# Attention products turned round: values stationary, probabilities moving, row sums divided out by a diagonal in the transposes

## The reference, cut to what matters

```python
proj = rmsnorm(x, g_mix) @ w_in            # q_a, k_a, v_a, c_q, c_kv, k_pe, gate_a, gate_b
y_a = moba_attention(q_a, k_a, v_a)        # 8 heads of 64; with 256 tokens: one causal block
y_b = causal_attention(q_b, k_b, v_b)      # 8 heads, 96 features in q and k, 64 in v
# each head: probs = softmax(where(causal, q @ k.T * scale, -inf)); y = probs @ v
merged = sigmoid(gate_a) * (y_a @ w_branch_a) + sigmoid(gate_b) * (y_b @ w_branch_b)
x = x + merged @ w_out
x = x + routed_experts(rmsnorm(x, g_ffn), ...)   # top 4 of 32, every expert's 12 MB read
```

## Time and profile before

| | |
|---|---|
| median of 3 runs | 1439.06 us (1436.78 to 1440.57) |
| the profiled execution's own time | 1436.58 us |
| its span in the profile | 1434.2 us |
| PE busy in the span | 1360.7 us (95%) |
| DVE busy | 423.4 us (30%) |
| ACT busy | 274.7 us (19%) |
| mean HBM traffic | 348 GB/s |

### The profile page before, as it was taken

How to read it: one execution, slowest core, us unless ns; L and a number is a source line. 1 busy time by engine, 2 the same in 40 slices (tenths; PEclk the granted TensorE clock), 3 DMA queues, 4 the chain that set the end, 5 groups by cost and what they waited for, 6 DMA issues and landing times.

```text
span 1434.2 us, 16180 instructions
## 1 busy us (share of the span) xinstructions
PE 1360.7 (95%) x6618; PEld 678.6 (47%) x6618; DVE 423.4 (30%) x661; ACT 274.7 (19%) x392; POOL 30.7 (2%) x50
## 2 busy tenths in 40 slices
PE   8999999999999999999999898999999989999898
PEld 4446644433433343343333333333333336898896
DVE  2344323311211121121112111121112116775774
ACT  2133213110110111111101011010111114532531
POOL 2100010000000000000000000000000000000000
PEclk9999999999999999999999999999999999999999
DMA  9992377899999999999999999999999996355330
GB/s 329 387 341 88 118 265 321 361 416 426 429 428 428 429 429 428 429 428 428 429 428 430 428 430 427 429 429 428 430 428 429 428 413 238 126 179 199 122 124 30
DMA packets 76972, 498.71 MB, mean 348 GB/s; under 512 B 7095, under 2 KB 8586, under 8 KB 52362
## 3 DMA queue, kind: packets, MB, share of 16 engines
q1 hardware_dynamic: 75802, 496.06, 84.6%
q0 software_dynamic: 704, 2.10, 0.4%
q10 hardware_dynamic: 432, 0.07, 0.0%
HBM read 497.06 MB, written 1.05 MB: 347 GB/s over the span
## 4 chain that ended last, share of the span: by engine, by line
PE 69%; DMA 24%; DVE 4%; ACT 2%; issue 1%; POOL 0%; SPq 0%; ACTq 0%; DVEq 0%
PE ps L1621 31%; DMA ring<-in_w_gate_up_dram 24%; PE ps L1386 7%; PE ps L1731 5%; PE ps L1733 5%; PE ps L1732 5%; PE ps L1615 3%; PE ps L1552 2%; PE ps L1536 2%; PE ps L1396 2%; PE ps L1602 1%; PE ps L1686 1%; ACT arena L688 1%; PE ps L1625 1%; PE ps L1365 1%
## 5 line engine op out<-in xcount | busy, mean ns | idle before, releaser
L1621 PE MATMUL ps<-ring,arena 128*64 128x512 f32 x2304 | 515.3, 598 | 28.2 <-DMA ring<-in_w_gate_up_dram 17.1
L1621 PEld LDWEIGHTS ps<-ring,arena 128*64 128x64 f32 x2304 | 159.5, 137 | 356.5 <-issue 304.7
L1621 PE MATMUL ps<-arena 128*64 128x512 f32 x768 | 177.9, 616 | 5.0 <-ACT arena L688 3.1
L1130 DVE TENSOR_SCALAR arena<-ps 128x512 f32<-128x512 f32 x32 | 22.1, 692 | 342.5 <-PE ps L1621 342.5
L681 ACT ACTIVATE arena<-arena 128x512 f32<-128x512 f32 x32 | 20.2, 630 | 491.4 <-DVE arena L1130 491.4
L1386 PE MATMUL ps<-ring,HT 128*128 128x512 f32 (+1 forms) x256 | 111.3, 586 | 1.3 <-ACT HT L594 1.0
L1621 PEld LDWEIGHTS ps<-arena 128*64 128x64 f32 x768 | 54.2, 141 | 119.5 <-issue 105.0
L1733 PE MATMUL ps<-arena_highs,w_low 128*128 128x256 f32 x384 | 108.5, 282 | 0.0
L1091 DVE TENSOR_SCALAR esel<-const 128x128 fp32r<-128x128 f32 x49 | 12.6, 285 | 281.4 <-ACT arena L692 143.5
L692 ACT COPY arena<-ps 64x512 f32<-64x512 f32 x64 | 37.1, 580 | 241.0 <-PE ps L1621 240.6
L1109 DVE TENSOR_TENSOR X<-X,ps 128x1024 f32<-128x1024 f32 x34 | 41.4, 1218 | 121.5 <-PE ps L1615 121.5
(11 more groups left out here) (246 smaller groups left out, 1341.2 us busy)
## 6 DMA issues: line engine op xcount, KB each, us to landing
ring<-in_w_gate_up_dram SPq DMA_DIRECT2D x96, 2048.0 KB, 31.0
ring<-in_w_down_dram SPq DMA_DIRECT2D x48, 2048.0 KB, 33.7
arena<-in_w_gate_up_dram SPq DMA_DIRECT2D x32, 2048.0 KB, 30.7
ring<-in_w_in_dram SPq DMA_DIRECT2D x38, 1024.0 KB, 6.9
arena<-in_w_down_dram SPq DMA_DIRECT2D x16, 2048.0 KB, 34.3
ring<-in_w_ada_dram SPq DMA_DIRECT2D x24, 1024.0 KB, 13.3
ring<-in_w_out_dram SPq DMA_DIRECT2D x12, 1024.0 KB, 6.3
ring<-in_w_ple_gate_dram SPq DMA_DIRECT2D x4, 1024.0 KB, 27.0
```

Source lines behind the costliest of these rows:

```text
L1621: last = T.matmul(ps[at:at + CAP, bank, :], lhsT, w(g), start=False, stop=stop)
```

## The change

The two products of a head are turned round. In PV the head's 64 columns of values become the stationary operand and the transposed probabilities the moving one (256 columns for the keys of the first half, 128 for those of the second), so the result has features on partitions, in PSUM partitions 0 to 63 for even heads and 64 to 127 for odd ones. Since queries are then columns, the row sums can't be divided out per partition at the end. They are divided out in the transposition: `shares_of_rows(h)` on DVE takes the reciprocals of the head's two columns of sums and multiplies the identity by them, and T becomes an ordinary fp32 product of the probabilities (stationary) with that diagonal (moving). The 16 transposes of the result, `normalise` and the moves `yTa` and `yTb` go; ACT copies the result of each branch from PSUM to `yT` (the memory of `HN`), after PV(7) and after PV(15). The raw expert biases are loaded to the memory of `HT`, which POOL may do as soon as the last gate projection has been made.

```diff
-            moved(pool, "yTb")
+            pool.wait_ge(s["chunk_used1"], used1("gb1"))
...
+            def out_of_attention(br):
+                act.wait_ge(s["pv_done"], HEADS * (br + 1))
+                A.copy(yT[:, 4 * br:4 * br + 4, :].rearrange("p a b -> p (a b)"), flat(3)).then_inc(s["y_done"], 1)
...
                 if h == HEADS - 1:
+                    out_of_attention(0)
...
-            move("yTa", HT[:, 0:4, :].rearrange("p a b -> p (a b)"), flat)
-            move("yTb", HT[:, 4:8, :].rearrange("p a b -> p (a b)"), flat)
+            moved(act, "gb1")
+            out_of_attention(1)
...
-            def normalise(br):
-                dve.wait_ge(s["pv_done"], HEADS * (br + 1))
-                r = st[:, 64 + 16 * br:80 + 16 * br]
-                run(V.reciprocal(r, r))
+            def shares_of_rows(h):
+                c = 64 + h // HEADS * 16 + h % HEADS
+                sums = st[:, c:c + 9:8]
+                dve.wait_ge(s["prob_done"], h + 1)
+                run(V.reciprocal(sums, sums))
                 join()
-                V.tensor_tensor(HN[:, br, :].rearrange("p (a d) -> p a d", d=HD),
-                                flat(3).rearrange("p (a d) -> p a d", d=HD),
-                                r.unsqueeze(2).to_broadcast([P, 16, HD]), ALU.mult).then_inc(s["y_done"], 1)
+                both = [P, HALVES, P]
+                V.tensor_tensor(shares_of[h // HEADS][:, h % 2], ident.unsqueeze(1).to_broadcast(both),
+                                sums.unsqueeze(2).to_broadcast(both), ALU.mult).then_inc(s["shares_in"], 1)
...
                     if h > h0:
+                        shares_of_rows(h - 1)
                         out_of_t(h - 1)
...
-                pe.wait_ge(s["prob_done"], h + 1)
+                pe.wait_ge(s["shares_in"], h + 1)
...
-                    last = T.transpose(ps[:, bank, b * P:b * P + P], prob[:, h % 2, b * P:b * P + P], ident)
+                    last = T.matmul(ps[:, bank, b * P:b * P + P], prob[:, h % 2, b * P:b * P + P],
+                                    shares_of[h // HEADS][:, h % 2, min(b, 1), :], start=True, stop=True)
...
-                T.matmul(ps[:, 6, c:c + HD], pt[:, 0:P], v(0), start=True, stop=True)
-                T.matmul(ps[:, 7, c:c + HD], pt[:, P:2 * P], v(0), start=True, stop=False)
-                T.matmul(ps[:, 7, c:c + HD], pt[:, 2 * P:3 * P], v(1), start=False, stop=True
-                         ).then_inc(s["pv_done"], 1)
+                at, bank, n = HD * (h % 2), 6 + h % HEADS // 4, h % HEADS // 2 % 2 * S
+                T.matmul(ps[at:at + HD, bank, n:n + S], v(0), pt[:, 0:S], start=True, stop=False, skip_group_check=True)
+                T.matmul(ps[at:at + HD, bank, n + P:n + S], v(1), pt[:, S:S + P], start=False, stop=True,
+                         skip_group_check=True).then_inc(s["pv_done"], 1)
...
-            for br, name in enumerate(("yTa", "yTb")):
-                pe.wait_ge(s["y_done"], br + 1)
-                p = free(pe, name)
-                if br:
-                    pe.wait_ge(s["t_free"], 2 * HEADS)
-                features(p, lambda k, h: HN[:, br, h * 512 + k * P:h * 512 + k * P + P]).then_inc(full1[p], 1)
...
-                    moved(pe, "yTb" if br else "yTa")
+                    pe.wait_ge(s["y_done"], br + 1)
```

More of the change, by code:

```diff
@@ L167, in build @@
         kTb = view(16, HEADS * S, "p (a b) -> p a b", a=HEADS)
+        yT = hn_flat.rearrange("p (a b) -> p a b", a=KC)
         latT = [view(70, S), view(71, S), view(60, S)]
@@ L177, in build @@
         merged = kv
+        shares_of = [view(28, 512, "p (b h n) -> p b h n", b=2, h=HALVES), view(44, 512, "p (b h n) -> p b h n", b=2, h=HALVES)]
         SQ = view(56, HALVES * 768)
@@ L195, in build @@
         pickw = view(20, HALVES * 3 * CAP, "p (h v b) -> p h v b", h=HALVES, v=3)
-        raw_bias = hn_flat[:, 512:2048]
+        raw_bias = ht_flat[:, 0:3 * 512]
         more_bins = [view(32, 2 * SLOT, "p (a b) -> p a b", a=2), view(56, 2 * SLOT, "p (a b) -> p a b", a=2)]
@@ L237, in build @@
         x_sums mod1_full mod1_moved c_sigmoid cwide_zero cwide_ready q_ready k_ready mlaq_ready mlak_ready
-        s_full s_free scored prob_done t_full t_free pv_done y_done
+        s_full s_free scored prob_done shares_in t_full t_free pv_done y_done
         gates_open merged_done half_out x_half wr_gained ffn_sums fT_high fT_low rt_full lg_ready mask_done expd pos_full
@@ L285, in build @@
                              ("qTb0", 2, N), ("qTb1", 0, N), ("kTb0", 1, N), ("mod0", 0, N), ("kTb1", 2, N),
-                             ("gb0", 2, used1("gb0")), ("gb1", 2, used1("gb1")), ("yTa", 2, N), ("yTb", 0, N),
+                             ("gb0", 2, used1("gb0")), ("gb1", 2, used1("gb1")),
                              ("A0", 1, used1("A0")), ("B0", 2, used1("B0")), ("A1", 0, used1("A1")),
@@ L957, in _ @@
                         mla_step(h)
-                normalise(h0 // HEADS)
             dve.wait_ge(s["gates_open"], 2)
@@ L1535, in _ @@
                         for k in range(4):
-                            last = T.matmul(ps[:, 2 * p + h, :], HT[:, 4 * br + k, h * P:h * P + P],
+                            last = T.matmul(ps[:, 2 * p + h, :], yT[:, 4 * br + k, h * P:h * P + P],
                                             slot1(c, 4, 512)[:, k, :], start=k == 0, stop=k == 3)
```

## The result

The kernel after takes 1446.53 us (median of 4 runs, 1445.97 to 1448.32), the kernel before 1437.92 us (4 runs, 1436.48 to 1440.57). The ratio is 1.0058, with an interval of 1.0042 to 1.0073: slower by 8.6 us (6.0 to 10.5 by the interval). The profiled execution of after took 1446.54 us (before 1436.58), its span is 9.8 us longer.

What follows compares the result with a forecast made beforehand. PE was taken to bound the head loop, its delay moving every later load. Terms 5.3 + 4.8 + 0.9 + 0.8 - 0.4 + 0.1 - 2.75 = +8.8 us gave 1447 us, range 1441.5 to 1451.5.

Steps and rivals of the forecast that it cites:

- The delay passes whole: From attention to the end: loads wait for PE, so a PE delay moves every later load and the end equally.
- T's second pass: T in each of 16 heads: six instructions and 0.66 us instead of 0.33, +5.3 us in all.
- rival (e): T in the head loop takes four times as long, 1.32 us: together +19, 1457 us; chance 0.03.
- The diagonal on DVE: Hidden in MLA turns; T waits for it in three MoBA turns, +0.9 us, and at both branch ends, +0.8.
- The circle: MoBA branch: T(h-2), copy, MLA step, score, diagonal, T(h-1) through DVE; 6.53 us once, 6.22 twice, against PE's 6.06.
- The end of the attention: Between PV(15) and the first branch product, transposes and the wait for normalise go: -2.75 us.
- ACT, +0.1: ACT's copy after PV(7) fills a 2.42 us wait; the first qTb move may slip by some 0.1 us.
- PV, +4.8: PV in both branches: moving columns as good as unchanged, but each tile shape change costs 0.19 us; +4.8 us in all.
- rival (a): Changes of tile shape at PV cost nothing: +4.3 us, 1443; chance 0.14.
- Rival (c): PV gets cheap by overlapping its neighbour, 5.1 us less, no shape cost: -2.5 us, 1436.5; chance 0.06.
- Rival (b): Nearly no change: shape costs nothing and DVE's circle and tail are hidden; +2.5 us, 1441.5; chance 0.08.
- Rival (d): Semaphores and diagonals on DVE 0.3 us dearer, shape changes 0.25 us: +11.8 us, 1450 to 1451; chance 0.10.

Runs made afterwards that it cites:

- The idle products: The kernel after with 16 idle 512-column products of PE ahead of the branch products: 1459.98 us, ratio to before 1.0149.
- one-pass kernel: The kernel after with T as a plain transposition that still waits for DVE's diagonal, division left out: 1440.7 us in one execution.
- kernel without the diagonal: The kernel after with T a two-pass product with the identity, no diagonal or division: 98.54 us from first scores to first branch product (after 100.70).
- kernel with padded values: Probabilities scaled in place on DVE, one-pass T, each head's values zero-padded to 128 columns, full result: 1438.08 us, ratio to before 0.999.
- probabilities scaled in place: The kernel after with DVE multiplying probabilities by the reciprocals, T a one-pass transpose, PV 64 wide, full result: 1441.67 us, ratio to before 1.0022.
- kernel with the diagonal earlier: The kernel after with DVE making head h's diagonal in turn h, not h+1: 98.84 us from first scores to first branch product (after 100.70).

## Why the prediction was right

Direction, size and place were right: 1447.0 was forecast, 1446.53 measured; in the attention +8.8 forecast, +7.94 measured. By its steps:

- **The delay passes whole.** The idle products, 13.84 us of PE, lengthen the span by 13.6 us. The reading behind it was thinner than the result: the earlier trace rows shows one early window with the DMA engines at 0.37, and others nearby are full (before has 1.00 at 270 to 280 us). What carries the step is SP's waiting for PE.
- **T's second pass, +5.3.** The runs give 16 x 0.34 = 5.4: three instructions become six, as the row of the diagonal product had it, and of PE's own work only T is shorter in the one-pass kernel. The Trainium skill (TensorE: Matmul & The Clock Gate, Terms) has four times for fp32; these traces disagree, it is twice, and rival (e) falls.
- **The diagonal on DVE, +0.9 and +0.8.** Measured 2.2, the difference to the kernel without it. The circle was sized closely: 6.53, 6.22 and 6.22 us forecast, 6.56, 6.15 and 6.15 measured, the ends of the branches 2.06 and 2.02. PE's own turn, from which the wait counts, is 5.94 and not the 6.06 of the prediction, since shape is cheaper there. So the five turns are 1.25 us longer in all instead of 0.9, and the two ends 0.47 each instead of 0.38. Two of the five turns, 6.05 and 6.04 us, were not forecast to be longer at all: a T that has waited takes 0.87 us to its PV (112.80 to 113.67) instead of 0.76, and that falls into the next turn.
- **The end of the attention, -2.75.** Measured -2.70.
- **ACT, +0.1.** The copy takes 1.01 us from 135.54 and the moves behind it start at 136.55. From the first transposes behind the branch to the first scores of the MLA branch it is 5.22 us (135.44 to 140.66) instead of 5.19: next to nothing.
- **A wait that was overlooked, 0.35.** I took all MoBA turns of before as 5.42 us. One is 5.77, with 0.30 us of waiting for ACT. After it is gone, and no term of the sum had it.
- **PV, +4.8, is the mis-sized term**, with its -0.4 for the wait before PV(15) +4.4. The kernel without the diagonal is 98.54 - 92.76 = 5.78 us above before; less 5.44 for T's pass, plus 2.70 for the end and 0.35 for the lost wait, PV keeps 3.39 us. T's starts say the same: the ten turns with a PV give 2.5 us where I had 3.6, the ends of the branches 0.9 where I had 0.8. An MLA turn pays 5.75 - 5.09 - 0.34 = 0.32 where I had 0.41, a MoBA turn 5.94 - 5.42 - 0.34 = 0.18 where I had 0.31. The step at fault is the price of one change of shape, 0.19 us, taken from four 512-column instructions in the expert stage and set twice in each turn. The runs have 0.34 us in an MLA turn, spread over four places (0.10, 0.04, 0.09, 0.10), and 0.14 in a MoBA turn, whose scores have a shape of their own anyway; together 3.1 us where I had 4.5.

So the attention adds up: 5.44 + 2.16 + 3.39 - 0.35 - 2.70 = 7.94 us.

The Trainium skill (TensorEngine Tiling (Array Packing), Key Properties) says that PE drains when the tiling mode changes. The traces agree in so far as the same columns take 0.34 us less in a turn at full width, and rival (a) falls by it. They do not show the drain itself, and the 0.10 us inside the scores, between two products of one shape, is not at a border. Rival (c) falls as well: L1493 and L1494 stand one behind the other in 0.79 us, no pair overlaps. Rival (b) falls with shape and the circle. Rival (d) falls too, though the waits are longer than priced: it needs a circle of 0.3 us more in three turns, and the circle came as sized.

The total was nearer than its terms had a right to, and that is luck. PV was 1.0 us too dear and a wait of 0.35 us was overlooked; the waits for DVE, 0.5 us too cheap, took part of that back. 1447 stood on a base of 1447 - 8.8 = 1438.2, the base in these runs was 1437.9, and the attention gave 7.9 of the 8.6 us. The 0.7 us between are less than the interval of the ratio and less than the 2.7 us by which single profiles scatter behind the attention; they stay open. The times of rivals (a) to (c) in the prediction stand on 1439.06 and not on 1438.2, some 0.9 us higher than the forecast's own base; it changes nothing here.

## What to carry over

To fold a scaling into a transposition on TensorE is not free in fp32: the product doubles the instructions (0.33 to 0.67 us for three blocks). A multiply in place on DVE cost PE nothing in the MLA turns (5.41 us, as in the one-pass kernel), where DVE rests; in the MoBA turns, where it does not, it came back as a wait of 1.5 us through ACT until the order there was changed. If a result is wanted with its features on partitions, keep the stationary operand at full width, with zeros in the unused half, rather than half a tile among full ones: the MLA turn is 5.09 us instead of 5.41. And work that another engine takes over must be placed by what it waits for in that engine's queue: the diagonals, 0.6 us each, cost 2.2 us in all only because they stood behind work of other heads. When PE gets faster, the same wait grows.

## What the runs showed of the hardware

The clock fell after a short pause, in one execution. In the kernel with padded values PE paused 1.81 us at 109 to 111 us, and the window behind shows a granted clock of 0.57 of full speed, so mostly the lower of the two levels (1.2 instead of 2.4 GHz); PE was busy throughout the window. With probabilities scaled in place PE paused 1.53 us at the same place, and the window behind it shows 1.00. Why the one fell and the other did not, these traces don't show. The two windows, each in its own kernel (columns as above):

```profile
112.00:116.00 4.00, 4.00 (x7) 1.55 (x6) 2.67 (x7) 0.99 (x4) 1.97 (x1) 0.57 0.36 138
```

```profile
111.40:115.40 4.00, 4.00 (x12) 1.87 (x13) 3.71 (x8) 0.15 (x1) 0.91 (x1) 1.00 0.64 246
```

The fall cost 5.37 - 3.70 = 1.7 us there, as much as the pause itself.

The first products of the program have two paces. Before, and then the kernel with the diagonal earlier:

```profile
9.24 7.10 PE L1386 MATMUL ps<-ring,HT 128*128 128x512 f32 x16 [0.96 <-ACT HT L594]
```

```profile
9.22 7.03 PE L1396 MATMUL ps<-ring,HT 128*128 128x512 f32 x11 [0.96 <-ACT HT L596]
```

The same instructions, 16 in 7.1 us or 11 in 7.0, with a granted clock of 1.00 in the window of 9 to 16 us of either; the first 32 take 14.0 us or 15.8 to 16.4. Everything behind starts some 2 us later (the first scores at 86.1 or at 88.0 to 88.7 us). Six of the twelve profiles have the one pace and six the other, and one execution of a kernel by itself tells nothing below 2 us for this reason. What causes it, these traces don't show.
